# Summing a recurrence's decays by scans along the free axis, and multiplying them into the streams one stage earlier

## The reference

```
proj = h @ w_in                                  # 768 tokens (256 context, 512 latent), 1024 channels
r, k, v, lw, la = centred token shift of proj     # g = 1024 more columns, not shifted
w_raw = w0 + tanh(lw[d]) @ w2[d]                  # d = 0, 1: direction
decay = exp(-exp(-softplus(-w_raw) - 0.5))        # = exp(-exp(-0.5) * sigmoid(w_raw))
a  = sigmoid(a0 + la[d] @ a2[d])
kk = k * k_k, normalised per head of 64;  kd = k * (1 + (a - 1) * k_a)
per step: S = S * decay - (S kk) (kk a)^T + v kd^T;   o = S r
```

## Time and profile before

| | us |
|---|---|
| median of 3 runs (lowest, highest) | 2942.53 (2935.29, 2944.64) |
| the profiled execution, its own time | 2946.32 |
| its span in the profile | 2944.2 |

### The profile page before, as it was taken

The page is one execution under the profiler, slowest core; times in us unless marked ns, Lnnn a source line. Parts: engine busy times, 40 slices in busy tenths (PEclk is TensorE's granted clock), DMA queues, the critical chain, the costliest instruction groups (busy, mean ns, idle before and its releaser), DMA issues.

```text
span 2944.2 us, 59653 instructions
## 1 busy us (share of the span) xinstructions
PE 2405.3 (82%) x25912; PEld 1729.5 (59%) x25912; DVE 1299.1 (44%) x2249; ACT 1141.8 (39%) x1918; POOL 959.0 (33%) x730
## 2 busy tenths in 40 slices
PE   8598897388888878877598888868599999699999
PEld 2576675266766767656465555535455556455556
DVE  0445464144445555543354454451444542444542
ACT  1444344143344444432343444332344442344442
POOL 0334444311122131214343333333443442443432
PEclk9799999699999999998799989978899998899999
DMA  6233434532232222122111011103011112111112
GB/s 241 79 106 121 138 99 125 171 121 74 74 107 86 74 62 84 41 100 91 63 44 36 29 33 32 36 7 122 29 51 43 51 51 68 40 51 43 51 51 65
DMA packets 100052, 220.00 MB, mean 75 GB/s; under 512 B 33360, under 2 KB 52048, under 8 KB 98896
## 3 DMA queue, kind: packets, MB, share of 16 engines
q1 hardware_dynamic: 88496, 172.93, 18.4%
q0 software_dynamic: 10144, 40.11, 4.2%
q10 hardware_dynamic: 1152, 3.15, 0.3%
HBM read 173.95 MB, written 42.21 MB: 73 GB/s over the span
## 4 chain that ended last, share of the span: by engine, by line
PE 54%; DVE 15%; POOL 12%; ACT 7%; issue 7%; DMA 4%; POOLq 0%; SPq 0%; ACTq 0%; DVEq 0%
PE ps L263 7%; PE ps L264 6%; PE ps L265 6%; PE ps L1264 2%; DMA s_bg_dram<-gbuf 2%; PE ps L485 2%; PE ps L1279 2%; PE ps L1254 2%; PE ps L2598 2%; POOL wbl L248 2%; PE ps L1055 2%; PE ps L2149 2%; PE ps L2112 2%; PE ps L2620 2%; DVE Rc L324 1%
## 5 line engine op out<-in xcount | busy, mean ns | idle before, releaser
L248 POOL TENSOR_TENSOR wbl<-wb,wbh 128x1024 fp32r<-128x1024 f32 x128 | 310.3, 2424 | 419.6 <-ACT wbh L243 413.6
L263 PE MATMUL ps<-hT2h,wbh 128*128 128x512 f32 x448 | 198.9, 444 | 52.9 <-POOLq L335 51.2
L263 PE MATMUL ps<-hTh,wah 128*128 128x512 f32 (+1 forms) x544 | 201.8, 371 | 29.8 <-POOLq L335 29.8
L263 PE MATMUL ps<-hT1h,wbh 128*128 128x512 f32 (+1 forms) x448 | 186.7, 417 | 36.9 <-DMA ac<-in_ac 31.8
L264 PE MATMUL ps<-hTl,wah 128*128 128x512 f32 (+1 forms) x544 | 185.9, 342 | 0.0
L265 PE MATMUL ps<-hTh,wal 128*128 128x512 f32 (+1 forms) x544 | 185.4, 341 | 0.0
L265 PE MATMUL ps<-hT2h,wbl 128*128 128x512 f32 x448 | 178.7, 399 | 0.0
L264 PE MATMUL ps<-hT2l,wbh 128*128 128x512 f32 x448 | 178.5, 398 | 0.0
L243 ACT ACTIVATE wbh<-wb 128x1024 fp32r<-128x1024 f32 x128 | 134.1, 1049 | 105.8 <-PE ps L265 49.4
L1157 POOL COPY pcs<-ARI 128x4 f32<-128x4 f32 x48 | 7.5, 187 | 492.4 <-ACT ARI L1135 492.4
L248 POOL TENSOR_TENSOR wal<-wa,wah 128x1024 fp32r<-128x1024 f32 x34 | 85.4, 2511 | 251.8 <-ACT wah L243 251.8
(11 more groups left out here) (387 smaller groups left out, 6074.0 us busy)
## 6 DMA issues: line engine op xcount, KB each, us to landing
wb<-in_w_in SPq DMA_DIRECT2D x56, 512.0 KB, 3.5
wm<-in_ada SPq DMA_DIRECT2D x48, 512.0 KB, 4.4
s_str_dram<-s POOLq DMA_DIRECT2D x48, 448.0 KB, 7.1
wa<-in_rw_in SPq DMA_DIRECT2D x34, 512.0 KB, 3.5
wb<-in_da_in SPq DMA_DIRECT2D x32, 512.0 KB, 3.5
ld<-s_str_dram SPq DMA_DIRECT2D x24, 512.0 KB, 5.2
ld<-s_str_dram SPq DMA_DIRECT2D x48, 256.0 KB, 5.2
wb<-in_w_out SPq DMA_DIRECT2D x16, 512.0 KB, 3.5
```

The source lines that it names most:

```text
L248: e.tensor_tensor(self.lo[:, n % 2], self.raw[:, n % 3], self.hi[:, n % 2].bitcast(F32), ALU.subtract).then_inc(self.K.s.w_lo, 1)
L263: e.matmul(z, wh[:, k, :], hi[:, k, a:b], start=k == 0, stop=False)
```

## The change

The decays are now made group by group inside `post`, with channels on partitions. Per group and direction PE makes w_raw in the same layout as everything else (two matmuls, `pe_decays`), ACT adds w0 as a bias and takes the sigmoid into tile wp, whose chunks are 65 columns apart (one gap column each). DVE sums along the free axis with one scan instruction of 780 columns per direction, a multiplication by `keep` (0 at the gaps, 1 elsewhere) starting each chunk anew; the backward direction takes the chunk's total minus the sum. ACT makes the exponentials of both signs (four instructions), DVE multiplies five of eight products, POOL three, and POOL also copies the chunk-end decays to a small tile pcA that stays in SBUF. The stream tile has nine rows instead of seven (kk and r are now different for the two directions), so each store is larger. The `sg` array, its 12 stores, and the decays at group 1 and beside the last post are gone. `post` has 8 steps instead of 7. Tile ss has one buffer instead of two, so DVE waits for its own previous mix.

In Scan, `cum` is gone on all engines. SP's fetch writes r and kk products straight into ARI and the other three into bkv, in eight DMAs with runs of 256 and 512 bytes; it waits until step u-2's matrices are made and the inversion of u-4 has read ARI.

```diff
-        self.lw2, self.w0b = K.sb(c, "lw2", [4, 1024]), K.sb(c, "w0b", [2, 1024])
+        self.lw2 = K.sb(c, "lw2", [2, 1024])
...
-        self.s7 = [K.sb(c, f"s7{i}", [7, NT]) for i in range(2)]
+        self.s9 = [K.sb(c, f"s9{i}", [9, NT]) for i in range(2)]
...
+        if m:
+            e.wait_ge(s.mix_done, m)
         e.tensor_tensor(ss[:, 0:769], pad[:, 0:769], pad[:, 2:771], ALU.add).then_inc(s.mix_sum, 1)
...
+    def pe_decays(self, e, gp, d):
+        s, n = self.K.s, 4 * gp + 2 * d
+        for j, (a, b) in enumerate(self.cols):
+            if n:
+                e.wait_ge(s.sg_sig, n + j - 1)
+            e.matmul(self.K.psum[:, 6 + j, 0:b - a], self.lw2[64 * d:64 * d + 64, 0, 128 * gp:128 * gp + 128],
+                     self.tl[64 * d:64 * d + 64, a:b], start=True, stop=True).then_inc(s.sg_mm, 1)
+
+    def act_decays(self, e, gp):
...
+        for d in range(2):
+            for j, (a, b) in enumerate(self.cols):
+                e.wait_ge(s.sg_mm, 4 * gp + 2 * d + j + 1)
+                K.table[0] = "sig"
+                e.activation(self.chunks(self.wp[:, d], 1, a, b), self.by_chunk(K.psum[:, 6 + j, 0:b - a]), ACT.Sigmoid,
+                             bias=K.Q("w0", 8 * d + gp, 1)).then_inc(s.sg_sig, 1)
...
     def pe_post(self, e, gp):
+        self.pe_decays(e, gp, 0)
         yield
         e.wait_ge(s.kk_sq, gp + 1)
         for j, (a, b) in enumerate(self.cols):
...
             self.rs.pe(e, 2 * gp + j, K.psum[:, 4 + j, 0:b - a], K.blk, sq[:, a:b])
+        self.pe_decays(e, gp, 1)
+        yield
+        yield
         yield
...
     def act_post(self, e, gp):
+        e.activation(sq, S9[:, 7, :], ACT.Square).then_inc(s.kk_sq, 1)
+        yield
+        self.act_decays(e, gp)
         yield
...
+        for d in range(2):
+            e.wait_ge(s.cum_v, 3 * gp + 1 + 2 * d)
+            K.exp_ln(e)
+            e.activation(self.inverse(d), self.before(d)[0], ACT.Exp, scale=DECAY).then_inc(s.dec_a, 1)
+            e.wait_ge(s.dec_a, 4 * gp + 2 * d + 1)
+            e.activation(self.er[:, d], self.er[:, d], ACT.Exp, scale=-DECAY).then_inc(s.dec_a, 1)
+        yield
...
     def dve_post(self, e, gp):
+        for d in range(2):
+            e.wait_ge(s.sg_sig, 4 * gp + 2 * d + 2)
+            e.tensor_tensor_scan((self.er if d == 0 else self.wp)[:, d], self.keep[:, :], self.wp[:, d], 0.0, ALU.mult,
+                                 ALU.add).then_inc(s.cum_v, 1)
+        e.wait_ge(s.cum_v, 3 * gp + 2)
+        c = self.wp[:, 1].rearrange("x (n t) -> x n t", t=65)
+        e.tensor_tensor(self.er[:, 1].rearrange("x (n t) -> x n t", t=65), c[:, :, 64:65].to_broadcast([128, 12, 65]), c,
+                        ALU.subtract).then_inc(s.cum_v, 1)
...
+        e.tensor_tensor(self.by_chunk(S9[:, 5, :]), self.by_chunk(kk), self.before(0)[1], ALU.mult).then_inc(s.prd_v, 1)
...
+        for z, d in ((0, 0), (3, 1), (4, 1)):
+            x = self.by_chunk(S9[:, z, :])
+            e.tensor_tensor(x, x, self.inverse(d), ALU.mult).then_inc(s.prd_v, 1)
+        yield
+        e.wait_ge(s.prd_v, 5 * gp + 1)
+        e.tensor_tensor(self.by_chunk(kk), self.by_chunk(kk), self.before(1)[1], ALU.mult).then_inc(s.prd_v, 1)
...
     def pool_post(self, e, gp):
+        e.wait_ge(s.dec_a, 4 * gp + 4)
+        for d in range(2):
+            m = e.tensor_copy(K.pcA[:, gp, 12 * d:12 * d + 12], self.er[:, d, 64 - 64 * d:780:65])
+        m.then_inc(s.prd_p, 1)
...
+        e.tensor_tensor(self.by_chunk(S9[:, 6, :]), r, self.before(0)[0], ALU.mult).then_inc(s.prd_p, 1)
+        yield
+        yield
+        e.wait_ge(s.bonus_v, 2 * gp + 1)
+        x = self.by_chunk(S9[:, 1, :])
+        e.tensor_tensor(x, x, self.inverse(0), ALU.mult).then_inc(s.prd_p, 1)
+        e.wait_ge(s.bonus_v, 2 * gp + 2)
+        e.wait_ge(s.prd_p, 4 * gp + 2)
+        e.tensor_tensor(r, r, self.before(1)[0], ALU.mult).then_inc(s.prd_p, 1)
         yield
         e.wait_ge(s.bonus_out, 2 * gp + 2)
-        e.wait_ge(s.kd_made, 6 * gp + 6)
+        e.wait_ge(s.prd_v, 5 * gp + 5)
+        e.wait_ge(s.prd_p, 4 * gp + 4)
         e.wait_ge(s.evac_a, 2 * (6 + 4 * gp))
         for n in range(6):
-            e.dma_start(K.T["str"][gp, n], self.s7[u][:, :, 128 * n:128 * n + 128]).then_inc(self.st_out[u], 16)
+            e.dma_start(K.T["str"][gp, n], S9[:, :, 128 * n:128 * n + 128]).then_inc(self.st_out[u], 16)
...
+        for gp in range(7):
+            pace((post(gp), 8), (project(gp + 1), 12))
+        run(post(7))
...
     def sp_fetch(self, e, u):
         if u >= 2:
 
-            e.wait_ge(s.pp_mm, self.pp_use[u - 2] + 2)
-            e.wait_ge(s.pr_v, 2 * (u - 1))
-            e.wait_ge(s.pr_p, 3 * (u - 1))
+            e.wait_ge(s.pp_mm, self.pp_use[u - 2] + 5)
+        if u >= 4:
+
+            e.wait_ge(*self.iv_at(u - 4, v=7))
         for d in range(2):
...
             for q in range(2):
+                e.dma_start(self.bkv[:, w, d, :, :, q, :], src[:, q, 2 * d:2 * d + 3, :].rearrange(
+                    "p n (c t) -> p n c t", c=2)).then_inc(self.scan_in[w], 16)
+                e.dma_start(self.ARI[:, q, i:i + 2, 128 * d:128 * d + 128],
+                            src[:, q, 5 + 2 * d:7 + 2 * d, :]).then_inc(self.scan_in[w], 16)
...
-    def pe_cum(self, e, u):
-    def act_cum(self, e, u):
-    def dve_cum(self, e, u):
-    def pool_cum(self, e, u):
```

More of the change, by code:

```diff
@@ L558, in __init__ @@
         self.sqb = K.sb(c, "sqb", [2, NT])
-        self.sgb = [K.sb(c, f"sgb{i}", [1024]) for i in range(2)]
+        self.wp, self.er = K.sb(c, "wp", [2, 780]), K.sb(c, "er", [2, 780])
+        self.keep = K.sb(c, "keep", [780])
         self.rs = Rstd(K, "ra", 16)
@@ L791, in act_decays @@
-    def act_decays(self, e):
-        K, s = self.K, self.K.s
-        for q in range(12):
-            e.wait_ge(s.sg_sum, 2 * q + 2)
-            K.table[0] = "sig"
-            e.activation(self.sgb[q % 2][:, :], self.sgb[q % 2][:, :], ACT.Sigmoid).then_inc(s.sg_sig, 1)
-            yield
-    def pool_decays(self, e):
-        K, s = self.K, self.K.s
-        for q in range(12):
-            d, n = divmod(q, 6)
-            e.wait_ge(s.sg_sig, q + 1)
-            e.dma_start(K.T["sg"][d, n], self.sgb[q % 2][:, :]).then_inc(self.sg_out[q % 2], 16)
-            yield
@@ L807, in together @@
-    def together(self, project, post, decays):
-        run(project(0))
-        dg = decays()
-        for gp in range(8):
-            if gp < 7:
-                fill = [(some(dg, 6), 6)] if gp == 1 else []
-                pace((post(gp), 7), (project(gp + 1), 12), *fill)
-            else:
-                pace((post(gp), 7), (dg, 6))
+    def together(self, project, post):
+        run(project(0))
+        for gp in range(7):
+            pace((post(gp), 8), (project(gp + 1), 12))
+        run(post(7))
@@ L892, in pool @@
                 e.memset(self.pads[i][:, cc:cc + 1], 0.0).then_inc(s.pad_zero, 1)
+        for d in range(2):
+            e.memset(self.wp[:, d, 0:780:65], 0.0).then_inc(s.cum_set, 1)
+        e.memset(self.keep[:, :], 1.0).then_inc(s.cum_set, 1)
+        e.wait_ge(s.cum_set, 3)
+        e.memset(self.keep[:, 0:780:65], 0.0).then_inc(s.cum_set, 1)
         for n in range(2):
             self.W.split_lo(e, n + 1)
-        self.together(lambda gp: self.pool_project(e, gp), lambda gp: self.pool_post(e, gp),
-                      lambda: self.pool_decays(e))
+        self.together(lambda gp: self.pool_project(e, gp), lambda gp: self.pool_post(e, gp))
         for u in range(2):
@@ L960, in __init__ @@
         n = Counter()
-        self.cum_use = {}
-        for u in range(-1, 24):
+        for u in range(24):
             if self.turn(u) is not None:
@@ L1604, in sp_bg, with together @@
         e.dma_start(self.bgl[:, :, :], self.K.T["bg"][gp]).then_inc(s.bg_in0, 16)
-    def together(self, cum, prepare, invert, chain, readout):
+    def together(self, prepare, invert, chain, readout):
         def prepared(u):
@@ L2933 @@
     put("a0", _np.concatenate([cols(I["rw_a0"][0, d]) for d in range(2)], axis=1))
+    put("w0", _np.concatenate([cols(I["rw_w0"][0, d]) for d in range(2)], axis=1))
     two = lambda v: _np.tile(v, 2)[:, None]
@@ L2963 @@
         T[k] = nc.dram_tensor("in_" + k, a.shape, _mybir.dt.float32, kind="ExternalInput").ap()
[L2964 removed]
+    for k, shape in (("str", (8, 6, 128, 9, 128)), ("bg", (8, 128, 2, 768)),
                      ("y", (128, 8, 768))):
```

277 lines of the change are left out of this document (98 added, 179 removed).

## The result

The changed kernel takes 3018.2 us (median of 4 runs, 3011.5 to 3021.8), the kernel before 2942.0: a ratio of 1.026, 95% interval 1.0234 to 1.0286. The forecast was 2962, range 2918 to 3010. The direction was right; the size was not, and the time lies outside the range.

The account below looks back on a forecast made before the run. Mix was taken as bound by a loop of release, store issue and landing with no engine full, Scan mostly by PE. Mix +92 and Scan -73 gave +19 on 2946.3, 2965, less 3.8 for the median: 2962, range 2918 to 3010.

Parts of the forecast that it names:

- The store issue at 38.8 + 4.4 + 1.8 = 45.0 us: Mix block, after the release: DVE chain 38.8, POOL splits 4.4, one POOL product 1.8; 30.7 before.
- The lock term: Mix: DVE stands still during POOL instructions; two of four splits 4.4 us, one of three products 1.8 us a block.
- Rival 2: Mix: lock takes more, three POOL products and a third split; store issue 50.8, Mix +130, Scan -61, 3011; chance 0.12.
- The scan term: Mix, DVE: two scans of 780 columns at 0.98 us each, 2.0 for both, before the bonus output.
- 6.5x - 200: Mix: the stage's added time in us, about, with x the first store issue in us after the release.
- Issue to landing: Mix block: from store issue to landing, 15.6 us before plus 2.6 for larger stores; 18.2 forecast.
- -73: Scan: whole-stage change in us, -50 summing matmuls, -11 start, -15 ACT and DVE work, +3 first fetch; bounds -92 and -53.
- these 15: Scan: ACT and DVE work leaving the chain in eight steps from 941.6, half of 31 us; bounds 0 and 31.
- The step of 26.7 us: Scan: step length before, read as 294.2 / 11; to fall to some 24 us as a sign.
- The serial start: Scan's beginning: sums, exponentials and POOL's products go; first transposes about 14 us after the barrier instead of 21.4.
- Rival 4: Scan: the fetch with small runs becomes the bound; at 30 us a fetch 73 us more; chance 0.03.
- Rival 1: Mix: store issue slips less as POOL fits DVE's gaps; issue at 38.8, Mix +52, 2921; chance 0.30 for this side.

Follow-up runs that it names:

- a_nolock: Changed kernel with POOL's three products cut to 64 of 768 columns and its Mix splits to 128 of 1024: 2948.9 us, ratio to before 1.0028.
- b_slope: Kernel before the change with five more 768-column multiplications on DVE (4.8 us) right ahead of the bonus output: 2977.2 us, ratio 1.0109.
- b_twice: Kernel before the change with Scan's summing matmuls L1055 issued twice, 1.94 us more PE time in each of 24 steps: 2994.3 us, ratio 1.0178.
- a_nosplit: Changed kernel with POOL's splits of the Mix weights cut to 128 of 1024 columns from the third on: 2989.1 us.
- a_noscan: Changed kernel with both DVE scans replaced by plain multiplications of the same tiles: 3000.6 us, ratio to before 1.0183.
- a_warm: Changed kernel with 48 more 512-column matmuls on PE while it waits for the store to land: 3015.9 us.

## Why the prediction was wrong

- **The store issue at 38.8 + 4.4 + 1.8 = 45.0 us is the step that failed.** It measured 50.6: start 10.2 (forecast 11.0), scans 2 x 1.78 = 3.6 (2.0), standing still for POOL 10.6 by the sum of its six stretches and 10.0 by a_nolock (6.2), and the rest 26.2 (25.2 without the scans' 2.0, plus 2.6: 25.8; in it L319 on 256 columns, 1.48 us beside POOL's norm step against 0.42 before). The stand-still is 4.4 too low, the scans 1.6 too low, the start 0.8 too high.
- **The lock term, the time in which DVE stands still for POOL.** I took two splits of four and one product of three because only two splits had hit DVE before. That was a count from an engine that was half idle. In a chain without gaps all three products and three splits hit it. Rival 2, with a chance of 0.12, had the true mechanism in Mix. That its numbers came close (x = 50.8, 3011) is in part luck: its stand-still of 12.0 was 1.4 too high and its scans 1.6 too low, and its Mix of +130 was 11 too low where its Scan of -61 gave 15 too little. The sentence on the Trainium skill, "SBUF — State Buffer", on engine ports and AXI ports, had the products right. By its rule the wait ends with POOL's instruction, and this trace agrees (L800: POOL ends at 406.48, DVE at 407.29, 0.8 us later; the instruction alone takes 0.95).
- **The scan term.** The row that I took, 0.98 us for the same shape in L604, is of another operation. The scan takes 1.78. The Trainium skill, "DVE: opcode table, instruction layouts, handler registers and perf-mode slots", section on datapath and trigger behaviour, gave half throughput, an estimate of 1.7; the trace agrees with it, with 1.78.
- **What a us of x costs: 6.5 was about right for added work.** b_slope cost 33 us for 4.8 in the medians, 6.9 each; in the profiled executions its Mix ended 29.2 us later (570.4 and 541.3), 6.1 each. a_nolock doesn't test the rule: its Mix ended 67.0 us sooner with x 7.1 lower in a steady block, because the first block, the two long blocks and the last post shrank by more. By 6.5x - 200 an x of 50.6 makes Mix +129; it was +140.6.
- **The clock explains most of the other 12 us, and I gave it no price.** In the block from 229.6 to 301.9 the sums, the decay matmuls and the twelve matmuls of the first product behind them all run at the lower of the two levels. The twelve start 0.43 us apart there and 0.23 in the steady block from 370.8. The decay matmuls and one of the twelve, first in that block and then in the steady one:

```profile
234.59 2.92 PE L677 MATMUL ps<-tl,lw 64*128 64x256 f32 x4
...
238.47 0.63 PE L260 MATMUL ps<-hTh,wal 128*128 128x512 f32 x1
```

```profile
375.73 1.66 PE L677 MATMUL ps<-tl,lw 64*128 64x256 f32 x4
...
377.89 0.39 PE L260 MATMUL ps<-hTh,wal 128*128 128x512 f32 x1
```

The first mix starts 14.0 us after the release instead of 10.2. The last interval between releases, 71.6, has the same pattern (first mix 13.3 after its release), and so has the block behind it: 3.8 + 3.1 + 3.1 = 10.0 us. I forecast a clock below 0.93 (0.85 here). In the terms: first release 7.3 us more than forecast, block two 9.4, four blocks 23.5, the tail 8.5: together 48.6 before rounding.
- **Issue to landing** 17.9 against 18.2, and the wait of ACT 16.6 for "well over 15": right.
- **Scan: -76 against -73, the sum right, the place in part luck.** L1055 is paid at 94% in the mean (b_twice). A step fell by 2.46 us in the mean; taking L1055's 1.94 off leaves 0.5 for the products behind it, 12 us over 24 steps where I took 15. But I had read these 15 in the stretch from 941.6, and there the gain was small: its ten steps, from QG to QG, fell from 29.4 to 28.1 us each, and the ten before them from 32.3 to 28.5. Why is open. The step of 26.7 us in the forecast is a misreading too: the stretch of 294.2 us holds ten steps, not eleven (QG at 941.70 and 1235.86), and so the step of 24 that was to show it did not come. The serial start: transposes 10.2 us after the stage's first load where 14 were forecast and 21.4 there before, because the fetch landed after 3.8 us and not late. Rival 4 falls: no wait for a fetch stands in the chain after the first.
- **Rival 1** needed DVE gaps for POOL's work; between the first mix and the store issue DVE has only 2.3 us of them, and in these it waits for POOL's norm steps.

Not settled: why PE's clock rises 3 us or more later after some releases than after others, though PE had waited nearly as long (12.1 us ahead of the sums at 441.39, 12.2 ahead of those at 509.88). It decides how much of a gain on DVE a block keeps: the late first mixes of a_nosplit, a_nolock and a_noscan all have it. a_warm shows only that filling the wait removes 1.0 us in a steady block and 9.2 over five, most of it where the late rise had been.

## What to carry to other kernels

When a block is a loop of release, work, store and landing, price an added instruction by the blocks it is in and not by its engine's idle share, and first look whether the wait that closes the loop stands earlier in program order than the write that it protects: moving it added no work and was worth 49 us before the change and 99 after it. Take such an edit into both kernels before judging a change: here the change costs 76 us with the early wait and 22 with the late one. Work given to POOL beside a busy DVE is not free: three products and three splits cost DVE 10 us of 40. And a busy time read at a clock of 0.93 is no floor.
